# A decoder trunk on one core: VectorE takes every fourth row of v beside the attention of the last four blocks, and one-trip loops become plain code

## What is computed

```python
h = rmsnorm(x);  x = x + hybrid_mixer(h)            # MLA attention, RG-LRU, differential attention
h = rmsnorm(x);  x = x + memory_cross_attention(h)
h = rmsnorm(x);  x = x + peer_ffn(h)                # the expert retrieval
...
# peer_ffn: 8 heads x 16 experts = 128 experts for each token
act = gelu(einsum('td,thkd->thk', x, u[experts]))
y   = einsum('thk,thkd->td', g * act, v[experts])
```

## Time and profile before

| | us |
|---|---|
| median of three runs | 3489.36 |
| the three runs | 3480.17, 3489.36, 3491.93 |
| span of the profiled execution, first to last instruction | 3488.4 |
| busy PE, DVE, POOL, ACT | 2948.9, 2349.6, 2015.7, 812.5 |

### The profile page before, as it was taken

The page is one execution under the profiler, slowest core; times in us unless marked ns, Lnnn a source line. Parts: engine busy times, 40 slices in busy tenths (PEclk is TensorE's granted clock), DMA queues, the critical chain, the costliest instruction groups (busy, mean ns, idle before and its releaser), DMA issues.

```text
span 3488.4 us, 34790 instructions
## 1 busy us (share of the span) xinstructions
PE 2948.9 (85%) x10984; PEld 1651.9 (47%) x10984; DVE 2349.6 (67%) x5893; ACT 812.5 (23%) x1915; POOL 2015.7 (58%) x2085
## 2 busy tenths in 40 slices
PE   7876898888988898889997899888998889976675
PEld 6465455544545355534554456444564445522222
DVE  6229846886588765886578765886648865596555
ACT  3111411132211421133211322114221232211111
POOL 1004755666566765666565655665556655477775
PEclk9898999999999999999999999998999999999998
DMA  7788999999999999999999999999999999999998
GB/s 279 277 274 313 408 409 409 408 409 409 409 407 406 394 409 409 408 407 382 409 409 408 392 356 409 409 409 348 359 409 409 409 355 342 385 404 410 409 409 347
DMA packets 386971, 1345.09 MB, mean 386 GB/s; under 512 B 41762, under 2 KB 44834, under 8 KB 386148
## 3 DMA queue, kind: packets, MB, share of 16 engines
q0 software_dynamic: 294912, 1073.87, 78.1%
q1 hardware_dynamic: 90724, 264.79, 20.0%
q10 hardware_dynamic: 1152, 4.19, 0.3%
HBM read 1332.99 MB, written 35.39 MB: 392 GB/s over the span
## 4 chain that ended last, share of the span: by engine, by line
PE 38%; DMA 30%; DVE 15%; POOL 9%; issue 6%; ACT 3%; SPq 1%; DVEq 0%; POOLq 0%; ACTq 0%
PE ps_sum L1267 18%; DMA rows<-in_peer_u,ids_u 13%; DMA rows<-in_peer_v,ids_v 10%; PE ps_p L999 5%; POOL rows L824 5%; POOL rows L810 4%; DVE rows L2052 4%; PE ps_s L1181 4%; DMA rows<-in_peer_v,ids_u 3%; DMA w_ring<-packed 3%; PE ps_s L1118 2%; PE ps_p L1126 2%; DVE feat_b L1935 1%; DVE feat_b L1931 1%; PE ps_s L1114 1%
## 5 line engine op out<-in xcount | busy, mean ns | idle before, releaser
L1267 PE MATMUL ps_sum<-rows,diag 128*128 128x512 f32 x3548 | 1727.6, 629 | 267.1 <-DMA rows<-in_peer_v,ids_v 141.4
L2052 DVE CUSTOM_DVE_ANT_0 rows<-h_cur,rows 128x1024 f32<-128x1024 f32 x1024 | 1226.8, 1220 | 496.3 <-DMA rows<-in_peer_u,ids_u 483.3
L810 POOL DMA_INDIRECT rows<-in_peer_u,ids_u x1024 | 1012.3, 989 | 702.0 <-issue 483.3
L1267 PEld LDWEIGHTS ps_sum<-rows,diag 128*128 128x128 f32 x3548 | 671.0, 200 | 1155.7 <-issue 1005.7
L824 POOL DMA_INDIRECT rows<-in_peer_v,ids_v x512 | 490.3, 958 | 433.8 <-PE ps_sum L1267 277.6
L824 POOL DMA_INDIRECT rows<-in_peer_v,ids_u x512 | 498.2, 973 | 284.7 <-PE ps_sum L1267 144.2
L1528 ACT ACTIVATE diag<-ident,acts 128x128 f32<-128x128 f32 x887 | 324.7, 394 | 1049.4 <-PE ps_sum L1267 750.1
L999 PE MATMUL ps_p<-hT,w_ring 128*128 128x128 f32 x2944 | 358.7, 282 | 28.8 <-DMA w_ring<-packed 15.3
L999 PEld LDWEIGHTS ps_p<-hT,w_ring 128*128 128x128 f32 x2944 | 353.0, 198 | 61.2 <-issue 39.7
L1834 DVE CUSTOM_DVE_ANT_0 e<-ps_s,bias_t 128x256 f32<-128x256 f32 (+6 forms) x96 | 74.2, 773 | 176.3 <-PE ps_s L1118 73.7
L2074 DVE SCALAR_TENSOR_TENSOR x_cur<-rows,acts,x_cur 128x1024 f32<-128x1024 f32 x137 | 175.6, 1282 | 7.4 <-DMA rows<-in_peer_v,ids_v 7.3
(11 more groups left out here) (288 smaller groups left out, 2376.2 us busy)
## 6 DMA issues: line engine op xcount, KB each, us to landing
w_ring<-packed SPq DMA_DIRECT2D x343, 512.0 KB
w_ring<-in_wstream SPq DMA_DIRECT2D x65, 512.0 KB
packed<-in_wstream SPq DMA_DIRECT2D x49, 512.0 KB, 8.2
rows<-in_peer_u,ids_u POOLq DMA_INDIRECT x1024, 14.9
rows<-in_peer_v,ids_u POOLq DMA_INDIRECT x512, 12.6
rows<-in_peer_v,ids_v POOLq DMA_INDIRECT x512, 19.3
bias_rows<-rows SPq DMA_DIRECT2D x5, 1024.0 KB, 12.1
bias_t<-in_x SPq DMA_DIRECT2D x8, 512.0 KB, 7.9
```

Source lines behind the costliest of these rows:

```text
L810: pool.indirect_dma_start(u_rows[:, slot, :], None, peer_u, bass.IndirectOffsetOnAxis(ap=ids_u[:, j:j + 1], axis=0)).then_inc(u_landed[slo ...
L1267: ins = pe.matmul(ps_sum[:, c * 512:(c + 1) * 512], diag[:, n % 4, :], v_rows[:, slot, c * 512:(c + 1) * 512], start=(j == 0), stop=(n == ...
L2052: dve.tensor_tensor_reduce(row, h_cur[:, :], row, 1.0, 0.0, ALU.mult, ALU.add, dots[:, p:p + 1]).then_inc(u_used, 1)
```

## The change

In the retrievals of blocks 3 to 6, which run beside the fronts of blocks 4 to 7, DVE adds also the v rows j = 11, 19, 27 and 35 (those with j % 4 == 3 from 10 to 41 that it did not add already). They are added at positions 24, 32, 40 and 48. That makes 16 rows that leave PE, with their 16 diagonals on ACT, and go to DVE. The stops stay as they are. The loops become plain code on four engines, and DVE's counted waits become waits on constants.

```diff
 def on_vector(b, j):
 
+    if LATE <= b < NB - 1 and CROWDED[0] <= j < CROWDED[1] and j % 4 == 3:
+        return True
     return j % SHARE == SHARE - 1 or (b == NB - 1 and j >= TAIL and j % 2)
...
+LATE = 3
+CROWDED = (10, 42)
...
-                with pe.Fori(first, last) as b:
+                for b in range(first, last):
...
-            scores_waited, keys_waited, top_waited = (counter(dve, n) for n in ("scores_waited", "keys_waited", "top_waited"))
+            waited = dict.fromkeys((s_ps, k_out, top_step), 0)
+
+            def wait_next(semaphore, n):
+
+                waited[semaphore] += n
+                dve.wait_ge(semaphore, waited[semaphore])
...
-                wait_more(dve, s_ps, scores_waited, 1)
+                wait_next(s_ps, 1)
...
-                    wait_more(dve, top_step, top_waited, n)
+                    wait_next(top_step, n)
```

More of the change, by code:

```diff
@@ L768, in _ @@
                     front["cross_q"] = lambda b: front_loads(b, per_tile * 25, per_tile * 33)
-                with sp.Fori(first, last) as b:
+                for b in range(first, last):
                     pace.run(stages(front, last=first == NB - 1), b)
@@ L1562, in _ @@
             for pace.body, (first, last, wide[0]) in enumerate(LOOPS):
-                with act.Fori(first, last) as b:
+                for b in range(first, last):
                     pace.start(b - 1)
@@ L1937, in top16 @@
                             dve.match_replace(s, v[:, 0:8], s, -3.0e38).then_inc(top_step, 1)
-                    wait_more(dve, top_step, top_waited, 2 * n if first == 0 else n)
+                    wait_next(top_step, 2 * n if first == 0 else n)
             def top(b, g):
                 pace.part(0.2)
-                wait_more(dve, k_out, keys_waited, 1)
+                wait_next(k_out, 1)
                 at = range(8 * g, 8 * g + 8)
@@ L1963, in choose @@
                                       ALU.add).then_inc(top_step, 1)
-                wait_more(dve, top_step, top_waited, 2)
+                wait_next(top_step, 2)
                 top16([best_v[:, h, :] for h in range(4 * g, 4 * g + 4)], [best_i[:, h, :] for h in range(4 * g, 4 * g + 4)],
@@ L2126, in _ @@
             for pace.body, (first, last, wide[0]) in enumerate(LOOPS):
-                with dve.Fori(first, last) as b:
+                for b in range(first, last):
                     steps.start(origin if first < 2 else b * block_steps + (origin - 2 * block_steps))
```

## The result

The kernel after takes 3491.05 us (median of 16 runs, 3482.40 to 3502.10) and the kernel before 3480.15 us in the 16 runs beside it (3473.62 to 3491.93). The ratio is 1.0025, with a 95% interval of 1.0013 to 1.0037: slower by 8.7 us [4.5 to 12.9], where 8 us less were forecast. The median does lie inside the forecast's 3464 to 3497 us, but that is luck: the three runs that the forecast started from had a median 9 us above that of the 16, and the change went the other way. The profiled execution of before, 3488.4 us long, was one of its slower ones, so the span after, almost the same, hides the loss.

What follows compares the result with a forecast made beforehand. It took PE to bind in the attentions of blocks 4 to 7, with room on DVE and full DMAs mostly elsewhere. Terms 0 + 2.3 + 4.3 + 0.7 + 3.2 + 0 - 2.5 = 8.0 us gave 3481 us, range 3464 to 3497.

Steps and rivals of the forecast that it cites:

- the clock's term: PE's longer wait in `mla_2` lowers the clock for one short stretch more in two blocks: 2.5 us lost, bounds 0 to 26.
- Position 24: v row 11 in `recur`, before the attention: PE gains nothing, DVE's extra work fits into waits; 0 us.
- Position 32: v row 19 in `mla_2`: mostly hidden beside the exponential; 1.1 us in block 6 and 0.3 per block, 2.3 us won.
- Position 40: v row 27 in `diff_0`: PE waits for ACT's second copy instead, 1.07 us won in each of four blocks, 4.3 us.
- Position 48: v row 35 in `diff_2`: DVE nearly full, attention's end moves +0.6, +0.1, -0.5, -0.9 us in blocks 4 to 7; 0.7 won.
- Constant waits: DVE's stops on the chain get shorter: 1.4 us in `mla_0` to `mla_2`, 1.8 us in block 0; 3.2 us won.
- Loops: Loop edges, 0.27 us on DVE, seven times on each engine, beside full DMAs: 0 us taken, bound 1.9 us won.
- The third one: Clock falls behind the new wait in `mla_2` in each of four blocks, costing 26 us: 3505 us; chance 0.09.
- The second: Rows at 24, 32 and 48 lie on DVE's path, 14.4 us lost: 3493 us; chance 0.14 with nothing seen.
- The first: Rows at 32, 40 and 48 give PE 1.72 us each, above 25 us in all: 3464 us; chance 0.27 with half.
- The fourth: Nothing seen, since full stretches after the attention give back PE's gain: 3489 us; chance 0.14 with DVE taking it back.

Runs made afterwards that it cites:

- after_again: The kernel after, unchanged, timed again beside the kernel before; ratio to before 1.0020.
- rows_only: The kernel before with the 16 rows moved to DVE, its loops and counted waits kept; ratio to before 1.0043.
- fill_19: The kernel after with a product by zeros on PE in the place of moved row 19 alone (position 32, `mla_2`), blocks 4 to 7; ratio to before 1.0002.
- plain_only: The kernel before with plain loops and constant waits alone, no v row moved to DVE; ratio to before 0.9992.
- plain_mla1: The kernel before with plain loops and constant waits, and the real row of position 31 before the turn in `mla_1`, blocks 4 to 7; ratio to before 0.9983.
- fill_zero: The kernel after with a product by zeros of the same shape on PE in the place of each of the 16 moved rows; ratio to before 0.9981.
- fill_rest: The kernel after with products by zeros on PE in the places of rows 11, 27 and 35, none in that of row 19; ratio to before 1.0002.
- fill_2735: The kernel after with products by zeros on PE in the places of rows 27 and 35 (positions 40 and 48) alone; ratio to before 1.0005.
- only_27: The kernel after with only v row 27 (position 40, `diff_0`) of each block's four moved to DVE; ratio to before 1.0003.
- only_19: The kernel after with only v row 19 (position 32, `mla_2`) of each block's four moved to DVE; ratio to before 0.9995.
- only_35: The kernel after with only v row 35 (position 48, `diff_2`) of each block's four moved to DVE; ratio to before 0.9990.
- fill_half: The kernel after with a full product by zeros in the place of row 19 and half of one in those of 27 and 35; ratio to before 0.9984.
- half_mla1: fill_half with the real row of position 31 placed before the turn in `mla_1`, blocks 4 to 7; 3464.82 us, ratio to before 0.9954.

## Why the prediction was wrong

**The step that failed** is the clock's term: "one short stretch more in two of the blocks, 2.5 us in all". In the two profiles it is (71.8 - 36.6) / 2 = 17.6 us. Over all profiles, the four with nothing in the places at 40 and 48 and at most one product put in (after, after_again, rows_only, fill_19) have 69.8 to 78.6 us at half clock, mean 73.9. The six with a full row or product in both places (before, plain_only, plain_mla1, fill_zero, fill_rest, fill_2735) have 22.5 to 36.6, mean 28.8. Half of the difference is 22.5 us, 20.0 more than I took. The timed executions fit this: over their whole length after_again's mean clock is 0.0055 below before's, some 38 us more at half clock, of which half is 19. The term was inside the bounds of 0 to 26, which I had from one long stretch, but I chose near the lower end, because block 4 had stayed at 1.00 behind the same wait. I had left block 5 out, where before has the wait too (2.48 us) and 3.4 us at half clock behind it, so it was three blocks of four. And I looked only at the long wait: the places at 40 and 48, where I counted a gain of 5.0 us, had no clock term at all, and there only_27 and after fall.

**Position 24** at nothing: as predicted. fill_zero and plain_only agree at full clock, so the row on DVE costs nothing there.

**Position 32** at 2.3 us: only_19 shows 2.3 at full clock, fill_rest 0.1. The size lies within what single profiles scatter.

**Position 40** at 4.3: only_27 shows 3.3. The wait in the row's place is 0.37, 0.47, 0.58 and 0.69 us in blocks 4 to 7 and was put at 0.65.

**Position 48** at 0.7: only_35 shows 5.5. The mechanism, a DVE without room for the row, was right in kind in blocks 4 and 5, where PE waits 0.90 and 0.36 us more for DVE (+0.6 and +0.1 predicted), and wrong in size in 6 and 7: 0.97 and 1.20 us of DVE's idle time are left. The 5.5 us rest on one profile with 65.4 us at half clock, so on the largest correction of the three. Together with 40, fill_19 against plain_only gives 9.8 where 5.0 were taken.

**Constant waits** at 3.2: plain_only's ratio says 2.8 us, with an interval from a gain of 7.3 to a loss of 1.4. At full clock its attentions are 0.9 us shorter (1.4 predicted) and the opening 4.7 (1.8 predicted).

**Loops** at nothing: the 0.27 us of the earlier trace rows are gone, and no run separates them from the waits. The Trainium skill ("Advanced Engine Details and Errata", Control Flow Timing) puts a compare-and-branch at some 108 ns and a branch at 51; the trace of before has 67 ns for the loops' compare-and-branch on PE and 43 on DVE.

With the measured terms the sum is 0 + 2.3 + 3.3 + 5.5 + 2.8 + 0 - 22.5 = -8.6: 8.6 us lost, against 8.7 [4.5 to 12.9] measured. So close an agreement is luck, since each gain in the attention rests on a single profile and the waits' on an interval of 9 us; that the clock's term outweighs all the others is not.

A slip of the prediction that changes nothing: half way between 3493 and 3505 is 3499, and the range ends at 3497.

**The rivals.** The third one had the sign, and its condition, 21 us more at 1.2 GHz, was met with 35 in the profiles. Its place was wrong. Half clock does stand behind the wait in `mla_2` in blocks 5 to 7, but filling it alone left as much half clock (78.6 us), and leaving it alone empty as little as with no hole (27.3 us). In time each of the two gave back some 0.2%. The second (DVE takes it back) is refuted by fill_zero, but for the short waits in blocks 4 and 5. The first (PE's time in full) holds at full clock by half: 10.8 us of 25. The fourth is excluded by the interval. The Trainium skill ("TensorE: Matmul & The Clock Gate", Why this matters for your kernels), whose rule on idle gaps between bursts I weighed and set aside, was right in direction. In these profiles two short waits (0.69 and 0.37 to 0.69 us) around the turns of `diff_0` and `diff_2` went with more half clock than a single one of 2.22 to 2.94 us in `mla_2`.

**What stays open.** Whether the clock follows the waits themselves or the lack of wide products around them is not separated. In fill_half half the work, with the wait closed, held it, which speaks for the wait; the pair in `mla_1` of half_mla1 at a clock of 1.00 speaks against the waits alone. By time the two places are not separated: filling row 19's alone gave 1.0002 and filling the other two 1.0005. fill_zero, fill_rest and fill_2735 have similar attentions at full clock (328.0 to 328.2), yet their ratios are 0.9981, 1.0002 and 1.0005. The mean clocks of their executions, 0.941, 0.939 and 0.939, would make up for it if the difference lay where PE binds: 0.002 less is some 15 us more at half clock, and half of that is 0.2% of the time. Where in the kernel it lies is not known, since the profiles show only one execution each. Why only_35, with 65.4 us at half clock in its profile, was timed at 0.9990 is open too, and so is why plain_only, with the fewest in its profile's attentions, has 0.939 over its executions and not before's 0.942. Where the clock falls differs from one execution to the next: 36.6 and 22.5 us in before and plain_only, which have the same rows.

## What to carry to other kernels

Where a bound engine's clock answers to its idle time, work taken from it has two prices: its time, and the wait that it covered. Before you move work away, look at what PE does just before and behind the place: if waits for a neighbour and short, narrow products are all that is left, the clock may fall there; leave something there that is as long as the wait and no longer, and put real work first into the waits that exist already. To find such a loss, put an empty product in each emptied place by turns, and compare windows at their granted clock; a sum of busy time can't show it, since busy time grows as the clock falls.

## What the runs showed of the hardware

A v row on DVE beside the attention cost nothing that shows in the sum at full clock (328.2 us in fill_zero and in plain_only), 16 of them, with DVE busy for 66 to 77% of the windows of fill_rest. A product with zeros kept the granted clock as a real one did (25.6 to 35.8 us at half clock, 22.5 to 36.6 with real rows). 64 matmuls fewer left PE as busy with rows as before (1726.4 us against 1727.6). And a few runs are a poor ruler here: before's three first runs had a median of 3489.36 us, its 16 runs 3480.15.
